# The first block's output projection with weights and operands split in high and low parts, in place of unsplit float32

## The chip, the cores and the metric

One core of a Trainium2 chip runs the whole program in one launch. The metric is the device time in microseconds; the kernel before has a median of 1708.94 us over 3 runs (1707.21 to 1710.25).

## The reference

A sequence of 256 tokens of width 1024, in float32, goes through two transformer-like blocks. The part that the change touches is the end of the first mixer of the first block:

```
y_a = gelu(z_gate) * rg_lru(xr, ...)                 # 256 x 1024, eight heads of 128
y_b = multi_scale_pool(z_pool, ...)                  # 256 x 512, four groups of 128
x = x + concatenate([y_a, y_b], axis=-1) @ w_out     # w_out is 1536 x 1024
```

Behind it come cross-attention (queries, scores, mix, output projection `wo0`), a gated feed-forward with a convolution, a conformer convolution block, a second cross-attention and feed-forward, and a second block with banded attention and a mixture of experts.

## The kernel before

All activations lie transposed: 128 channels on the partitions, 256 tokens along the free axis, so a tensor of width 1024 is eight chunks of 128x256. The weights come as one long stream of slabs, each 128x1024 float32 (512 KB), which SyncE loads into a ring of 12 places (`raw`). `S0` gives the first slab of each phase: `abin` (slab 0), `gk` (20), `v0` (32), `about` (40), `q0` (52), `wo0` (60). `about` is the output projection in question, with 12 slabs: the first four for the four pool groups, the other eight for the eight heads of the recurrence. A row slab holds 128 rows of the weight matrix; it gives eight products 128x128 by 128x256, one for each output chunk, which accumulate over the slabs of the phase in the eight half banks of `acc`.

**Two ways of multiplying.** For most phases ScalarE copies the raw slab to `wh` as float32r, the high part (line 699), and VectorE (line 1199) or GpSimd (line 1082) subtracts it from the raw slab to give `wl`, the low part: VectorE for slabs with an even split number, GpSimd for odd ones. The operand is in two parts in the same way (`yh` and `yl` for row slabs). TensorE then makes three float32r products for each float32 product, high by high, low by high and high by low (`tile3`, lines 1957 to 1959). `wh` and `wl` have four places (`SPLIT`), so a split waits until TensorE is done with the slab four back; splits are issued three slabs ahead (`AHEAD`). The phases `abin`, part of `gk`, `about` and `cw` are not split: `tile1` (line 1963) multiplies `raw` by the float32 operand, and the profile shows two records for each such product.

**The order around the change.** Every engine runs its own list in order, and they meet at counting semaphores. In the value phase `v0`, TensorE works on slabs 32 to 39. The first half (32 to 35) accumulates in banks `acc[2]` and `acc[3]`, which VectorE copies out in `v0_out(0)` (line 1370); the projection may not start before, as it uses the same banks:

```
            pe.wait_ge(S("v0_out"), TT)
            for n in range(12):
```

Meanwhile VectorE finishes the recurrence, one head after the other: a multiply (L1403), a scan (L1405) and a multiply with the gate (L1408), which leaves `y_a` of head n in `xr[:, n, :]` and raises `ya_ready`. `v0_out(0)` comes after head 4, `v0_out(1)` (line 1368) after head 7; in between stand the weight subtractions of slabs 36 and 38. `y_b` is in `z[:, 16 + g, :]` much earlier. In the projection TensorE waits for the raw slab and the operand alone; ScalarE, VectorE and GpSimd do little there except for the splits of slabs 52 to 54. When the last slab's chunks are done, VectorE adds them to the residual (`take_sums`, line 1253), ScalarE makes high parts `ah` of the next operand (L706), VectorE the low parts, and TensorE goes on with the first three query slabs (`lead`, lines 2042, 2043 and 2032). `row_slab`, the routine for split row slabs, runs already in `wo0` and later phases.

SyncE loads slab s into the place of slab s - 12: if that one is split, once its low part is made, otherwise once TensorE is done with it.

Of the kernel before, what the change touches and what calls it, by code (L numbers as in the profile page):

```python
# [31 lines left out]
F32 = mybir.dt.float32  # L32
# [206 lines left out]
def unsplit(s):  # L239

    if S0["gk"] <= s < S0["v0"]:
        return (s - S0["gk"]) % 3 == 0
    return s < S0["gk"] or S0["about"] <= s < S0["q0"] or S0["cw"] <= s < S0["cw"] + CW


def split_no(s):

    if s < S0["v0"]:
        return s - S0["gk"] - (s - S0["gk"] + 2) // 3
    if s < S0["about"]:  # L250
        return s - S0["gk"] - 4
    return s - S0["gk"] - 4 - 12 - (0 if s < S0["cw"] else CW)

# [62 lines left out]
def program(nc, stream, experts, cols_in, konst_in, masks_in, x_in, mem_in, router_in, out):  # L316
    ctx = ExitStack()
    with ctx:
# [366 lines left out]
        def _(act):  # L685
            A = Program(act, S("scalar_chain"))

            def split(s):
# [4 lines left out]
                if S0["v1"] <= s.base < S0["v1"] + SPLIT:  # L693
                    wait_slab(act, s + -(SPLIT + CW))
                elif S0["q0"] <= s.base < S0["q0"] + SPLIT:
                    wait_slab(act, s + -(SPLIT + 12))
                elif s.base >= S0["gk"] + SPLIT:
                    wait_slab(act, s + -SPLIT)
# [84 lines left out]
            for n in range(8):  # L783
                if n < 7:
                    split(At(S0["v0"] + n + 1 + AHEAD))
            for n in range(8):
                split(At(S0["about"] + n + AHEAD))
            act.dma_start(masks[:], masks_in).then_inc(S("masks_in"), 16)
# [285 lines left out]
        def _(pool):  # L1074
# [45 lines left out]
            splits(S0["gk"], 12)  # L1120
            splits(S0["v0"], 8)
            splits(S0["about"], 12)
# [68 lines left out]
        def _(dve):  # L1191
# [219 lines left out]
            v0_out(1)  # L1411
            splits(S0["about"], 11)
            take_sums("about")
# [539 lines left out]
        def _(pe):  # L1953
# [353 lines left out]
            for n in range(12):  # L2307
                s = At(S0["about"] + n)
                wait_raw(pe, s)
                if n < 4:  # L2310
                    wait_emptied(pe, USE0["gk"] + 5 * n + 2)
                else:
                    pe.wait_ge(S("ya_ready"), n - 3)
                for c in range(KC):
                    last = tile1(acc_of(c), s, c, z[:, 16 + n, :] if n < 4 else xr[:, n - 4, :],
                                 n == 0 and c % 2 == 0, n == 11, skip_group_check=True)
                    if n == 11 and c < KC - 1:
                        last.then_inc(acc_full, 1)
                last.then_inc(slab_done, 1)

# [505 lines left out]
```

## Time and profile before

| | us |
|---|---|
| median of 3 runs | 1708.94 |
| lowest, highest | 1707.21, 1710.25 |
| the profiled execution | 1709.44 |
| its span in the profile | 1707.6 |
| TensorE busy | 1635.0 (96%) |
| VectorE, ScalarE, GpSimd busy | 833.2, 603.8, 472.2 |
| unsplit matmuls of the projection (one piece of the chain) | 41.57 |

The span runs from the first to the last instruction that the profile shows. In the rows below PE is TensorE's matmuls, PEld its weight loads, DVE is VectorE, ACT ScalarE, POOL GpSimd, SP SyncE; L1963 is line 1963 of the kernel; `out<-in` names what is written and read; a time in brackets is how long the engine sat idle before the instruction, and what released it. Matmul records overlap, as they are pipelined, so the pace is the distance of two starts.

### The profile page before, as it was taken

What the parts mean: (1) busy time and instruction counts of PE and PEld (TensorE: products, weight loads), DVE (VectorE), ACT (ScalarE), POOL (GpSimd) and SP (SyncE); (2) the same over time, 40 slices, a digit from 0 to 9 for tenths busy, and PEclk for the clock granted to TensorE, in tenths of its full rate; (3) what the DMA queues carried; (4) which work ended last, traced back from release to release, by engine and by line L of the source; (5) the groups of instructions that cost most, each with busy time, mean ns of one, the idle gap of its engine ahead of it and who ended that gap; (6) DMA issues with size and microseconds to landing.
All of it is one profiled execution on the core that took longest, in us unless ns stands there. A gap on an engine that the chain in (4) does not pass through costs nothing.

```text
span 1707.6 us, 29356 instructions
## 1 busy us (share of the span) xinstructions
PE 1635.0 (96%) x11462; PEld 1294.7 (76%) x11462; DVE 833.2 (49%) x1397; ACT 603.8 (35%) x1019; POOL 472.2 (28%) x257
## 2 busy tenths in 40 slices
PE   7999999999999999999999999998799999999996
PEld 6898999999998799899999988887744443434332
DVE  2664457788873463888885436766501011010102
ACT  2371453443542444534444334655211111111101
POOL 1331424555543142355555342221200000000000
PEclk9999999999999999999999999999899999999998
DMA  7464634555568453455535664232979999999995
GB/s 290 149 222 154 212 109 149 185 172 184 185 177 247 165 182 118 138 180 181 177 127 161 228 190 136 98 104 102 370 297 421 421 421 422 422 421 422 421 422 212
DMA packets 85773, 401.06 MB, mean 235 GB/s; under 512 B 9520, under 2 KB 14000, under 8 KB 60848
## 3 DMA queue, kind: packets, MB, share of 16 engines
q1 hardware_dynamic: 84672, 395.81, 62.9%
q10 hardware_dynamic: 1008, 3.96, 0.6%
q8 instruction: 65, 1.06, 0.3%
q14 instruction: 28, 0.23, 0.0%
HBM read 394.02 MB, written 1.05 MB: 231 GB/s over the span
## 4 chain that ended last, share of the span: by engine, by line
PE 40%; issue 31%; DVE 23%; ACT 4%; POOL 1%; DVEq 1%; DMA 0%; ACTq 0%; SPq 0%; POOLq 0%
DVE wl L1199 5%; DVE cf L1517 5%; PE pw L1957 5%; PE pw L1959 5%; PE pw L1958 5%; PE pw L2270 4%; DVE hid L1533 3%; ACT wh L699 3%; DVE cf L1520 3%; PE acc L1963 2%; PE acc L1957 2%; PE acc L1959 2%; PE acc L1958 2%; PE acc L2129 2%; DVE gpad L1511 1%
## 5 line engine op out<-in xcount | busy, mean ns | idle before, releaser
L1082 POOL TENSOR_TENSOR wl<-raw,wh 128x1024 fp32r<-128x1024 f32 x157 | 388.3, 2474 | 579.9 <-ACT wh L699 576.2
L699 ACT ACTIVATE wh<-raw 128x1024 fp32r<-128x1024 f32 x314 | 325.0, 1051 | 245.3 <-PE pw L1959 108.5
L1957 PE MATMUL pw<-ah,wh 128*128 128x256 f32 x1272 | 364.4, 287 | 7.5 <-DVE gt L1690 4.0
L1958 PE MATMUL pw<-ah,wl 128*128 128x256 f32 x1272 | 359.8, 283 | 0.0
L1959 PE MATMUL pw<-al,wh 128*128 128x256 f32 x1272 | 359.7, 283 | 0.0
L1199 DVE TENSOR_TENSOR wl<-raw,wh 128x1024 fp32r<-128x1024 f32 x157 | 202.2, 1288 | 126.0 <-ACT wh L699 125.6
L1957 PEld LDWEIGHTS pw<-ah,wh 128*128 128x128 f32 x1272 | 243.6, 192 | 12.8 <-issue 10.5
L1958 PEld LDWEIGHTS pw<-ah,wl 128*128 128x128 f32 x1272 | 243.9, 192 | 0.1
L1959 PEld LDWEIGHTS pw<-al,wh 128*128 128x128 f32 x1272 | 243.8, 192 | 0.0
L1957 PE MATMUL acc<-yh,wh 128*128 128x256 f32 x672 | 194.8, 290 | 6.9 <-DVE yl L1729 2.8
L1958 PE MATMUL acc<-yh,wl 128*128 128x256 f32 x672 | 191.3, 285 | 0.0
L1959 PE MATMUL acc<-yl,wh 128*128 128x256 f32 x672 | 191.2, 285 | 0.0
L1093 POOL TENSOR_TENSOR small<-small 128x2 f32<-128x2 f32 x12 | 12.0, 1002 | 549.2 <-DVE small L1216 544.9
L1957 PEld LDWEIGHTS acc<-yh,wh 128*128 128x128 f32 x672 | 129.9, 193 | 10.0 <-issue 4.2
L1958 PEld LDWEIGHTS acc<-yh,wl 128*128 128x128 f32 x672 | 130.1, 194 | 0.1
L1959 PEld LDWEIGHTS acc<-yl,wh 128*128 128x128 f32 x672 | 130.0, 193 | 0.0
L1908 DVE COPY slot_gate<-pw 64x1 f32<-64x1 f32 x32 | 5.0, 156 | 245.7 <-ACT slots_to_tokens L1029 245.2
L2526 PE MATMUL pw<-raw,gathered 128*64 128x512 f32 x408 | 96.5, 601 | 3.5 <-DMA raw<-in_experts 2.0
L1517 DVE TENSOR_SCALAR cf<-gpad,cols 128x256 f32<-128x256 f32 x48 | 90.3, 1881 | 7.5 <-DVE gpad L1511 6.9
L2270 PE MATMUL pw<-x_gained,raw 128*128 128x256 f32 x320 | 74.4, 394 | 8.6 <-DMA raw<-in_stream 8.6
L852 ACT ACTIVATE cf<-cf 128x256 f32<-128x256 f32 x48 | 20.1, 418 | 164.5 <-DVE cf L1520 164.2
L1151 POOL TENSOR_TENSOR yl<-hid,yh 128x256 fp32r<-128x256 f32 x48 | 50.1, 1044 | 96.9 <-ACT yh L856 96.9
(315 smaller groups left out, 2601.8 us busy)
## 6 DMA issues: line engine op xcount, KB each, us to landing
raw<-in_stream SPq DMA_DIRECT2D x358, 512.0 KB, 3.3
raw<-in_experts SPq DMA_DIRECT2D x72, 1024.0 KB, 24.8
ring_w<-in_experts SPq DMA_DIRECT2D x47, 1024.0 KB, 26.7
ring_y<-in_experts SPq DMA_DIRECT2D x36, 1024.0 KB, 24.7
ring_m<-in_experts SPq DMA_DIRECT2D x24, 1024.0 KB, 24.8
ring_h<-in_experts SPq DMA_DIRECT2D x11, 1024.0 KB, 27.5
shifted<-hpad SPq DMA_DIRECT2D x16, 177.5 KB, 4.6
mem_t<-in_mem ACTq DMA_DIRECT2D x2, 1024.0 KB, 9.2
```

The lines of the kernel that those rows point to most:

```text
L699: A.done(act.activation(wh[:, s.base % SPLIT, :], raw[:, slot_of(s.base), :], ACT.Copy), w_hi)
L1082: G.done(pool.tensor_tensor(wl[:, s.base % SPLIT, :], raw[:, slot_of(s.base), :], wh[:, s.base % SPLIT, :].bitcast(F32), ALU.subtract), w_ ...
L1151: G.done(pool.tensor_tensor(yl[:, j % 4, :], hid[:, j % 2, :], yh[:, j % 4, :].bitcast(F32), ALU.subtract), S("ffn_hid_lo"))
L1199: V.done(dve.tensor_tensor(wl[:, s.base % SPLIT, :], raw[:, slot_of(s.base), :], wh[:, s.base % SPLIT, :].bitcast(F32), ALU.subtract), w_lo_v)
L1517: V.done(dve.tensor_scalar(cf[:, j % 2, :], gpad[:, j % 2, 2:T + 2], w, col(f"f_dw_b{l}", j, 4, i), ALU.mult, ALU.add))
L1520: V.done(dve.scalar_tensor_tensor(cf[:, j % 2, :], gpad[:, j % 2, 2 - k:T + 2 - k], w, cf[:, j % 2, :], ALU.mult, ALU.add), S("ffn_conv") ...
L1533: V.done(dve.tensor_tensor(hid[:, j % 2, :], cf[:, j % 2, :], uf[:, j % 2, :], ALU.mult), S("ffn_hidden"))
L1957: pe.matmul(dst, wh[:, s.base % SPLIT, w], hi, start=start, stop=False, **kw)
L1958: pe.matmul(dst, wl[:, s.base % SPLIT, w], hi, start=False, stop=False, **kw)
L1959: return pe.matmul(dst, wh[:, s.base % SPLIT, w], lo, start=False, stop=stop, **kw)
L2270: last = pe.matmul(pw[u % 4][:, 0:T], raw[:, slot_of(n), k * P:k * P + P], ax[:, k, :], start=(k == 0), stop=(k == KC - 1))
L2526: ins = pe.matmul(pw[bank + h][rows, :], stationary(e), expert_pair(s.base - S0["moe"])[:, e, 512 * h:512 * h + 512], start=first, stop=la ...
```

## The change

The twelve slabs of `about` are no longer exempt from splitting, and TensorE uses `row_slab` for them. ScalarE makes the high parts `yh` of the operands: of the four pool groups during the value phase, of the eight heads as they come, each followed by a weight split. GpSimd makes the low parts `yl` of the four pool groups, between its weight subtractions; VectorE makes those of the eight heads after `v0_out(1)`. The weight subtractions of slabs 40 to 51 go to VectorE (even) and GpSimd (odd), at the places where the lists call `split`: VectorE's of slab 40 stands before head 4, that of slab 42 before head 6. The load of the masks stays behind the same loop on ScalarE's queue, which has work in it now.

```diff
--- before.py
+++ after.py
@@ -240,16 +240,14 @@
 
     if S0["gk"] <= s < S0["v0"]:
         return (s - S0["gk"]) % 3 == 0
-    return s < S0["gk"] or S0["about"] <= s < S0["q0"] or S0["cw"] <= s < S0["cw"] + CW
+    return s < S0["gk"] or S0["cw"] <= s < S0["cw"] + CW
 
 
 def split_no(s):
 
     if s < S0["v0"]:
         return s - S0["gk"] - (s - S0["gk"] + 2) // 3
-    if s < S0["about"]:
-        return s - S0["gk"] - 4
-    return s - S0["gk"] - 4 - 12 - (0 if s < S0["cw"] else CW)
+    return s - S0["gk"] - 4 - (0 if s < S0["cw"] else CW)
 
 
 def ffn0(name):
@@ -692,8 +690,6 @@
                 wait_raw(act, s)
                 if S0["v1"] <= s.base < S0["v1"] + SPLIT:
                     wait_slab(act, s + -(SPLIT + CW))
-                elif S0["q0"] <= s.base < S0["q0"] + SPLIT:
-                    wait_slab(act, s + -(SPLIT + 12))
                 elif s.base >= S0["gk"] + SPLIT:
                     wait_slab(act, s + -SPLIT)
                 A.done(act.activation(wh[:, s.base % SPLIT, :], raw[:, slot_of(s.base), :], ACT.Copy), w_hi)
@@ -783,7 +779,12 @@
             for n in range(8):
                 if n < 7:
                     split(At(S0["v0"] + n + 1 + AHEAD))
+                if n < 4:
+                    wait_emptied(act, USE0["gk"] + 5 * n + 2)
+                    A.done(act.activation(yh[:, n, :], z[:, 16 + n, :], ACT.Copy), S("ab_hi"))
             for n in range(8):
+                act.wait_ge(S("ya_ready"), n + 1)
+                A.done(act.activation(yh[:, 4 + n, :], xr[:, n, :], ACT.Copy), S("ab_hi"))
                 split(At(S0["about"] + n + AHEAD))
             act.dma_start(masks[:], masks_in).then_inc(S("masks_in"), 16)
 
@@ -1118,7 +1119,12 @@
                     G.fence()
                     G.done(pool.tensor_tensor(z[:, 16 + g, :], src, z[:, 16 + g, :], ALU.subtract), S("pooled"))
             splits(S0["gk"], 12)
-            splits(S0["v0"], 8)
+            for n in range(8):
+                split(At(S0["v0"] + n + AHEAD))
+                if 1 <= n < 5:
+                    pool.wait_ge(S("ab_hi"), n)
+                    G.done(pool.tensor_tensor(yl[:, n - 1, :], z[:, 15 + n, :], yh[:, n - 1, :].bitcast(F32), ALU.subtract),
+                           S("ab_lo_pool"))
             splits(S0["about"], 12)
             for n in range(KC):
                 split(At(S0["q0"] + n + AHEAD))
@@ -1409,7 +1415,12 @@
                 if n == 4:
                     v0_out(0)
             v0_out(1)
-            splits(S0["about"], 11)
+            for n in range(11):
+                if n < 8:
+                    dve.wait_ge(S("ab_hi"), 5 + n)
+                    V.done(dve.tensor_tensor(yl[:, 4 + n, :], xr[:, n, :], yh[:, 4 + n, :].bitcast(F32), ALU.subtract),
+                           S("ab_lo_vector"))
+                split(At(S0["about"] + n + AHEAD))
             take_sums("about")
             split(At(S0["about"] + 11 + AHEAD))
 
@@ -2305,18 +2316,11 @@
                     value_slab(At(S0["v0"] + 4 * half + kk), kk, banks, mh, ml)
             pe.wait_ge(S("v0_out"), TT)
             for n in range(12):
-                s = At(S0["about"] + n)
-                wait_raw(pe, s)
                 if n < 4:
-                    wait_emptied(pe, USE0["gk"] + 5 * n + 2)
+                    pe.wait_ge(S("ab_lo_pool"), n + 1)
                 else:
-                    pe.wait_ge(S("ya_ready"), n - 3)
-                for c in range(KC):
-                    last = tile1(acc_of(c), s, c, z[:, 16 + n, :] if n < 4 else xr[:, n - 4, :],
-                                 n == 0 and c % 2 == 0, n == 11, skip_group_check=True)
-                    if n == 11 and c < KC - 1:
-                        last.then_inc(acc_full, 1)
-                last.then_inc(slab_done, 1)
+                    pe.wait_ge(S("ab_lo_vector"), n - 3)
+                row_slab(At(S0["about"] + n), n, n == 0, n == 11)
 
             def cross_layer(l):
                 lead(f"q{l}", f"xa{l}", f"q{l}")
```

## Rows read from the trace of the kernel before

**Rows 1.** The page, its first rows: span, busy time, share and instructions of TensorE.

```profile
span 1707.6 us, 29356 instructions
...
PE 1635.0 (96%) x11462; PEld 1294.7 (76%) x11462; DVE 833.2 (49%) x1397; ACT 603.8 (35%) x1019; POOL 472.2 (28%) x257
```

**Rows 2.** The chain that ended last, 100 to 200 us: start, duration, what.

```profile
142.19 41.57 PE acc L1963 x192
```

**Rows 3.** The waits, 120 to 190 us: who waited for whom, total, times, longest (us).

```profile
PEld acc L1963 <- DVE v_m L1370: 0.3, 1, 0.3
```

**Rows 4.** Timeline of TensorE, 131 to 257 us: start us, us, engine, line, op, out<-in, count.

```profile
131.15 0.39 PE L2091 MATMUL pw<-wh,mh 128*128 128x512 f32 x1
...
136.59 0.39 PE L2091 MATMUL pw<-wh,mh 128*128 128x512 f32 x1
...
142.05 14.08 PE L1963 MATMUL acc<-z,raw 128*128 128x256 f32 x64
...
183.41 0.47 PE L2042 MATMUL pw<-ah,wh 128*128 128x256 f32 x1
...
189.39 1.12 PE L2032 MATMUL pw<-al,wh 128*128 128x256 f32 x8
...
226.86 0.47 PE L1957 MATMUL acc<-yh,wh 128*128 128x256 f32 x1
...
250.08 0.28 PE L2042 MATMUL pw<-ah,wh 128*128 128x256 f32 x1
...
256.13 1.12 PE L2032 MATMUL pw<-al,wh 128*128 128x256 f32 x8
```

**Rows 5.** Timeline of VectorE, 122 to 142 us (same columns).

```profile
122.05 0.42 DVE L1334 COPY k_t<-pw 128x256 f32<-128x256 f32 x1
...
127.56 2.77 DVE L1405 TENSOR_TENSOR_SCAN z<-a_t,xr 128x256 f32<-128x256 f32 x1
...
131.35 0.69 DVE L1405 TENSOR_TENSOR_SCAN z<-a_t,xr 128x256 f32<-128x256 f32 x1
...
132.42 1.22 DVE L1199 TENSOR_TENSOR wl<-raw,wh 128x1024 fp32r<-128x1024 f32 x1
...
133.74 2.44 DVE L1403 TENSOR_TENSOR xr<-xr,z 128x256 f32<-128x256 f32 x1
...
139.19 0.43 DVE L1403 TENSOR_TENSOR xr<-xr,z 128x256 f32<-128x256 f32 x1
...
140.71 1.28 DVE L1370 COPY v_m<-acc 128x512 f32<-128x512 f32 x2
```

**Rows 6.** Timeline of GpSimd, 121 to 289 us (idle time and its releaser in brackets).

```profile
121.64 2.75 POOL L1082 TENSOR_TENSOR wl<-raw,wh 128x1024 fp32r<-128x1024 f32 x1 [2.92 <-ACT wh L699]
...
127.11 2.68 POOL L1082 TENSOR_TENSOR wl<-raw,wh 128x1024 fp32r<-128x1024 f32 x1 [2.72 <-ACT wh L699]
...
132.54 3.35 POOL L1082 TENSOR_TENSOR wl<-raw,wh 128x1024 fp32r<-128x1024 f32 x1 [2.76 <-ACT wh L699]
...
268.20 0.74 POOL L1151 TENSOR_TENSOR yl<-hid,yh 128x256 fp32r<-128x256 f32 x1 [3.39 <-ACT yh L856]
...
288.94 1.47 POOL L1151 TENSOR_TENSOR yl<-hid,yh 128x256 fp32r<-128x256 f32 x1 [2.98 <-ACT yh L856]
```

**Rows 7.** Timeline of ScalarE: a weight split, and an operand's high part.

```profile
125.97 1.06 ACT L699 ACTIVATE wh<-raw 128x1024 fp32r<-128x1024 f32 x1 [0.23 <-PE acc L2093]
...
267.70 0.42 ACT L856 ACTIVATE yh<-hid 128x256 fp32r<-128x256 f32 x1 [0.57 <-DVE hid L1533]
```

**Rows 8.** Timeline of TensorE: the first records after its two longest idle times.

```profile
8.59 5.71 PE L2270 MATMUL pw<-x_gained,raw 128*128 128x256 f32 x16 [8.59 <-DMA raw<-in_stream]
...
1230.15 0.63 PE L2502 MATMUL acc<-chosen,router_konst 128*128 128x32 f32 x2 [5.22 <-DVE chosen L1865]
```

**Rows 9.** Busy time of each engine by stretch, with TensorE's granted clock (PEclk), 1228 to 1230 us.

```profile
core 0: us, PE busy (x) PEld busy (x) DVE busy (x) ACT busy (x) POOL busy (x), PEclk, DMA share, GB/s
1228.00:1230.00 2.00, 0.00 (x0) 0.00 (x0) 1.97 (x15) 0.00 (x0) 0.00 (x0) 0.50 1.00 418
```

## The prediction

> **What bounds the kernel now.** The page comes first: TensorE is busy for 1635.0 of 1707.6 us [rows 1], so time is won or lost only where TensorE's own work or a gap in it changes. The chain that ended last, asked for the stretch of the output projection, gives one piece: 192 records of the unsplit matmul, 41.57 us without a break [rows 2]. A 128x256 float32 product leaves two records, so these are 12 slabs of 8 products, 0.433 us each. The waits name one stop at its door: TensorE waited 0.3 us for VectorE's copies out of the value sums [rows 3]. That small row matters most. The projection accumulates in the banks that these copies empty, and the copies stand in VectorE's queue behind five heads of the recurrence. VectorE had no slack there, and the change puts work in front of them.
>
> **TensorE's own work.** The row-slab routine already runs in the next projection: its eight slabs take 226.86 to 250.08 us. The first record is drawn out, so I go by records 0.12 us apart: 24 per slab, 2.88 us [rows 4]. Before, the run from 142.05 to 183.41 us [rows 4] gives 3.45 us a slab. Twelve slabs: 41.36 - 34.56 = 6.8 us gained, if everything arrives in time. A rule weighed against this: the Trainium skill (FP8 and Floating Point Precision, TensorE Precision Notes) says that true float32 takes 4 passes through the array. Counted as passes, three instead of four would give 31.0 us and a gain of 10.3, so the forecast below would be 3.5 us lower. The rows disagree: three split records cost 0.36 us against 0.433, a ratio of 0.83, and I keep the rows.
>
> **What is added to VectorE ahead of the value copies.** Calling the slabs of this projection 40 to 51 and the value slabs 32 to 39, VectorE now subtracts the low weights of slab 40 before head 4 (and those of 42 before head 6). One such subtraction is 1.22 us [rows 5], with its gap 1.3.
>
> **What GpSimd does to VectorE.** GpSimd gets four low parts of the pool operands and the low weights of slabs 41 and 43 in the same stretch. In the trace these operations and VectorE's operations with both inputs in SBUF exclude each other. The scan at 127.56 took 2.77 us and the multiply at 133.74 took 2.44, against 0.69 and 0.42 free, each ending 0.3 to 0.5 us after GpSimd's subtraction [rows 5, 6]. The reverse holds too: GpSimd's op at 132.54 took 3.35 us because VectorE's 132.42 was in flight. A copy out of PSUM at 122.05 ran in 0.42 us inside GpSimd's 121.64 to 124.39 and is not held. So a weight subtraction on GpSimd costs VectorE 2.0 us if it falls among the heads. An operand's low part is 0.74 us free and 1.47 when held [rows 6]; by the same reckoning (duration less 0.35) it costs VectorE 0.4.
> Do they fall there? ScalarE splits a slab 0.26 us after TensorE leaves the slab four back, for 1.06 us [rows 7]; value slabs last 2.72 us (131.15 to 142.05 for four [rows 4]). Slab 41 is ready for GpSimd at 136.59 + 0.26 + 1.06 = 137.9. Slab 43 waits for slab 39: with the small stop below, about 143.1 + 1.3 = 144.4. VectorE is then still in heads 2 to 4, so both hold it. The four operand parts come at 126 to 136 us, after ScalarE's 0.42 us copies [rows 7], and meet heads too.
> Sum: 1.3 + 2 x 2.0 + 4 x 0.4 = 6.9 us. Each of the ten or so handovers opens a few hundredths, and I take 7.2. The copies end at 140.71 + 1.28 + 7.2 = 149.2 instead of 142.0 [rows 5], and TensorE starts the projection 7.2 us late. The bounds: 1.3 if GpSimd's ops miss the heads or cost nothing, 9 if a third weight subtraction gets in.
>
> **A stop inside the value slabs.** The low weights of slab 38 began at 132.42. Three operand parts and the subtraction of slab 39 now come in ahead: 3 to 4 us later, done at 137.3 to 137.7, against 136.59, when TensorE wants them [rows 4]. That is 0.7 to 1.1 us, but it lies inside the 7.2, since TensorE then waits for the value copies anyway.
>
> **While the projection runs.** Per two slabs (5.76 us) GpSimd has 2.4 us, VectorE 1.22 + 2 x 0.42, together 4.5 when they exclude each other; ScalarE 2 x 1.48. Each fits. The first tight point is slab 44, whose operand VectorE makes only after heads 5 to 7 (3 x 1.7), slab 42 (1.3), the second pair of value copies (1.3), two operand parts (0.9), slab 44 itself (1.3) and one hold (2.0): 11.9 us after 149.2, so 161.1, where TensorE arrives at 149.25 + 4 x 2.88 = 160.8. A stop of 0 to 0.3 us, which the next term covers. The matmuls now wait for these low parts; nothing else on TensorE could run ahead of them.
>
> **The clock.** TensorE stands idle for some 6 us (143.1 to 149.2), longer than the 5.22 us before the router's counting [rows 8], where the granted clock stood at 0.50, the 1.2 GHz level, just before work resumed [rows 9]; and the first sixteen records of the kernel, after 8.59 us idle, took 5.71 us [rows 8], where 0.2165 us a record [rows 2] would give 3.46. That is 2.2 us lost there. I take 1.8, since fewer records of the shorter kind come first; the bounds are 0 and 3.5 (the full idle here is shorter, but nothing says how fast the clock returns).
>
> **The far end.** The three lead slabs of the queries, fed by the sums through VectorE and ScalarE, took 183.41 to 189.39 after the unsplit slab, and 250.08 to 256.13 after a split one [rows 4]: 0.07 us more. The four-back waits of ScalarE for slabs 51 to 54 end 1.3 us into the last slab, just ahead of the first sum. SP's loads of slabs 52 to 63 now follow the split of the slab in their slot, at about 145 for the first, where slab 40's end (145.5) released it; no later, and the splits of 52 come 30 us after. ScalarE's load of the masks slips from 131 to past 170 us; they are used only by the second block's attention. ScalarE was idle there, and its 12 splits and 12 copies (12 x 1.48 us) fit.
>
> **Sum.** 7.2 - 6.8 + 0.07 + 1.8 = +2.3 us. The profiled execution took 1709.44 us; it becomes 1711.7. That run lies 0.5 above the median of 1708.94, so I forecast 1711.2 for the median. Nothing behind absorbs a shift: TensorE goes straight on.
>
> **Rivals.** A measurement here can tell about 0.2%, 3.4 us.
> - *The forecast*: late value copies eat the gain. 1711.2, its own range 1709.5 to 1713. Chance 0.45, of which 0.08 lies past 1712.4.
> - *The clock does not fall, or only one of the two weight subtractions holds VectorE*: 2 us less each, 1707.5 to 1709.5. For it: both prices come from other places of the kernel. Against it: the two idles of rows 8 both left a mark. 0.20, within 0.2%.
> - *Slower, through the clock*: after the idle, TensorE stays at the lower level for 3.5 us more than it would, and slabs 44 to 46 come late too because GpSimd holds VectorE again. It decides once more than 2.8 us are lost to clock and stops together: 7.2 - 6.8 + 0.07 + 3.5 + 1 = +5, 1713.9. For it: at 1228 to 1230 the clock had already fallen with the idle [rows 9]. The Trainium skill (TensorE: Matmul & The Clock Gate, Part 1) calls the throttled state the default that activity releases, which agrees with that row. 0.25.
> - *Faster*: GpSimd's operations slip past the heads (they meet the copies, which are not held), the value copies end 1.3 us late, and the gain of 6.8 stands: 1.3 - 6.8 + 0.1 = -5.4, 1703.5. Against it: three of three weight subtractions on GpSimd in rows 6 met a VectorE op. 0.10.
> That the split matmuls would not run as such is excluded: the routine is the one of rows 4.
>
> **Numbers.** Faster 0.10; slower 0.25 + 0.08 = 0.33; the same 0.57. The range 1706.8 to 1714.8 takes in the second case and most of the third, and leaves out the fourth and a tail above.
>
> **What would show it.** Right: TensorE's wait for the value copies (before: 0.3 us) is 5 to 7 us, the copies end near 149 us, VectorE's ops among the heads show 2 us and more four times instead of twice, twelve slabs at 2.88 us after the first, a granted clock of 0.5 somewhere in 147 to 153. Wrong: a projection that starts before 145 us (then the kernel is faster), waits for low weights beyond slab 44 of more than a microsecond in sum (then slower), or a slab spacing other than 2.88.

## The result and the profile after

The changed kernel takes 1712.30 us in the median of 15 runs (1710.62 to 1713.55), beside 1709.21 for 15 runs of the kernel before (1707.21 to 1711.46). The ratio is 1.0016 [1.0009, 1.0023], or +3.1 us, slower by a little less than the 0.2% named in the prediction. The forecast was +2.3 us. A second comparison later gave 1.0010 [1.0001, 1.0019], or +1.7 us. The profiled execution took 1711.19 us, 1.8 us more than the profiled one before.

The page of the changed kernel answers to [rows 1]:

```profile
span 1709.4 us, 29608 instructions
PE 1630.8 (95%) x11558; PEld 1295.8 (76%) x11558; DVE 854.6 (50%) x1411; ACT 620.1 (36%) x1043; POOL 491.2 (29%) x267
```

TensorE is busy for 4.2 us less and the span is 1.8 us longer, so about 6 us of new idle time must lie somewhere. The waits of TensorE between 120 and 195 us (in total, times, longest, in us) name it:

```profile
PE acc L1968 <- DVE v_m L1376: 5.8, 1, 5.8
PE pw L2102 <- DVE wl L1205: 0.6, 1, 0.6
```

In place of the 0.3 us of [rows 3] TensorE waits 5.8 us for the value copies, and 0.6 us for the low weights of slab 38. No other wait of this stretch ended on low parts. TensorE's timeline shows both, and what follows (start, duration, line, operation, and in brackets the idle time and its releaser):

```profile
136.18 0.50 PE L2102 MATMUL pw<-wh,mh 128*128 128x512 f32 x1 [0.56 <-DVE wl L1205]
...
141.53 0.39 PE L2104 MATMUL pw<-wh,ml 128*128 128x512 f32 x1
147.75 0.58 PE L1968 MATMUL acc<-yh,wh 128*128 128x256 f32 x1 [5.83 <-DVE v_m L1376]
148.13 0.41 PE L1969 MATMUL acc<-yh,wl 128*128 128x256 f32 x1
...
150.48 0.38 PE L1968 MATMUL acc<-yh,wh 128*128 128x256 f32 x1
150.69 0.28 PE L1969 MATMUL acc<-yh,wl 128*128 128x256 f32 x1
150.81 0.28 PE L1970 MATMUL acc<-yl,wh 128*128 128x256 f32 x1
...
183.69 0.28 PE L2053 MATMUL pw<-ah,wh 128*128 128x256 f32 x1
```

This execution reached the stretch early: the low weights of slab 36 are made at 124.64, against 125.77 us before. So 1.13 us has to be added to its times to compare them. The head start arose ahead of anything that the change touches: the execution before shows a granted clock of 0.50 from 36.6 to 40.0 us, where that of the changed kernel shows 1.00.

```profile
36.60:40.00 3.40, 3.40 (x10) 2.64 (x9) 0.98 (x4) 0.60 (x1) 1.54 (x3) 0.50 0.39 133
```

The line gives the window, its length, the busy times of PE, PEld, DVE, ACT and POOL with their instructions, the granted clock, the busy share of the DMA engines and GB/s.

The projection starts at 147.75 + 1.13 = 148.88, against 142.05 before [rows 4], 6.8 us late. Its first twelve records are 0.21 to 0.38 us apart (2.73 us in all), the rest 0.12. It lasts 183.69 - 147.75 = 35.94 us, against 41.36 [rows 4]: 5.4 less. The stage as a whole is thus 6.8 - 5.4 = 1.4 us longer.

VectorE's timeline answers to [rows 5] and GpSimd's to [rows 6]. The first is VectorE's:

```profile
125.98 0.78 DVE L1409 TENSOR_TENSOR xr<-xr,z 128x256 f32<-128x256 f32 x1
126.79 2.77 DVE L1411 TENSOR_TENSOR_SCAN z<-a_t,xr 128x256 f32<-128x256 f32 x1
129.59 0.78 DVE L1414 TENSOR_TENSOR xr<-z 128x256 f32<-128x256 f32 x1
130.48 0.78 DVE L1409 TENSOR_TENSOR xr<-xr,z 128x256 f32<-128x256 f32 x1
...
132.01 2.44 DVE L1414 TENSOR_TENSOR xr<-z 128x256 f32<-128x256 f32 x1
134.38 1.75 DVE L1205 TENSOR_TENSOR wl<-raw,wh 128x1024 fp32r<-128x1024 f32 x1
...
137.42 2.44 DVE L1414 TENSOR_TENSOR xr<-z 128x256 f32<-128x256 f32 x1
...
141.50 1.22 DVE L1205 TENSOR_TENSOR wl<-raw,wh 128x1024 fp32r<-128x1024 f32 x1
142.82 0.43 DVE L1409 TENSOR_TENSOR xr<-xr,z 128x256 f32<-128x256 f32 x1
143.28 2.76 DVE L1411 TENSOR_TENSOR_SCAN z<-a_t,xr 128x256 f32<-128x256 f32 x1
146.07 0.42 DVE L1414 TENSOR_TENSOR xr<-z 128x256 f32<-128x256 f32 x1
146.42 1.28 DVE L1376 COPY v_m<-acc 128x512 f32<-128x512 f32 x2
```

And GpSimd's, with the low parts of the operands (L1126) among the weights (L1083):

```profile
126.44 2.58 POOL L1083 TENSOR_TENSOR wl<-raw,wh 128x1024 fp32r<-128x1024 f32 x1
128.96 2.00 POOL L1126 TENSOR_TENSOR yl<-z,yh 128x256 fp32r<-128x256 f32 x2
131.42 2.75 POOL L1083 TENSOR_TENSOR wl<-raw,wh 128x1024 fp32r<-128x1024 f32 x1 [0.46 <-ACT wh L695]
134.13 0.92 POOL L1126 TENSOR_TENSOR yl<-z,yh 128x256 fp32r<-128x256 f32 x1
136.86 2.72 POOL L1083 TENSOR_TENSOR wl<-raw,wh 128x1024 fp32r<-128x1024 f32 x1 [1.82 <-ACT wh L695]
143.15 2.34 POOL L1083 TENSOR_TENSOR wl<-raw,wh 128x1024 fp32r<-128x1024 f32 x1 [3.57 <-ACT wh L695]
```

Each of these weight subtractions on GpSimd has a stretched operation of VectorE beside it. Those of slabs 41 (136.86) and 43 (143.15) are new, and hold a multiply for 2.44 - 0.42 = 2.02 us and a scan for 2.76 - 0.69 = 2.07. The low parts of operands hold it for less: the multiplies at 125.98, 129.59 and 130.48 take 0.78 each where their like takes 0.42, and the subtraction at 134.38 takes 1.75 where others take 1.22.

The windows of the changed kernel show the granted clock behind the five busy times: 0.50, the 1.2 GHz level, while the projection starts, and 1.00, the 2.4 GHz level, for the rest of it.

```profile
147.26:150.68 3.42, 2.93 (x13) 2.93 (x14) 3.14 (x6) 0.00 (x0) 0.00 (x0) 0.50 0.02 5
150.70:183.60 32.90, 32.90 (x276) 32.90 (x276) 21.12 (x27) 14.92 (x21) 12.55 (x5) 1.00 0.61 207
```

### The profile page after: what moved, and what is told of

It reads as the page before. It is cut to its first block, busy times and chain, and to the rows that moved or that the text cites. A ratio compares the mean times of both kernels' runs of the same rounds, so it can differ in the third digit from the quotient of the medians.

```text
span 1709.4 us, 29608 instructions
## 1 busy us (share of the span) xinstructions
PE 1630.8 (95%) x11558; PEld 1295.8 (76%) x11558; DVE 854.6 (50%) x1411; ACT 620.1 (36%) x1043; POOL 491.2 (29%) x267
## 4 chain that ended last, share of the span: by engine, by line
PE 39%; issue 31%; DVE 24%; ACT 4%; POOL 1%; DVEq 1%; DMA 0%; ACTq 0%; SPq 0%; POOLq 0%
DVE wl L1205 6%; DVE cf L1528 5%; PE pw L1968 5%; PE pw L1969 5%; PE pw L1970 5%; PE pw L2281 4%; DVE hid L1544 3%; ACT wh L695 3%; PE acc L1968 3%; DVE cf L1531 3%; PE acc L1970 3%; PE acc L1969 3%; PE acc L2140 2%; DVE gpad L1522 1%; PE pw L2053 1%
## 5 line engine op out<-in xcount | busy, mean ns | idle before, releaser
L1083 POOL TENSOR_TENSOR wl<-raw,wh 128x1024 fp32r<-128x1024 f32 x163 | 402.9, 2472 | 561.8 <-ACT wh L695 558.1
L695 ACT ACTIVATE wh<-raw 128x1024 fp32r<-128x1024 f32 x326 | 337.8, 1051 | 256.5 <-PE pw L1970 108.7
L1205 DVE TENSOR_TENSOR wl<-raw,wh 128x1024 fp32r<-128x1024 f32 x163 | 210.1, 1290 | 130.1 <-ACT wh L695 129.4
L1968 PE MATMUL acc<-yh,wh 128*128 128x256 f32 x768 | 222.9, 290 | 12.8 <-DVE v_m L1376 5.8
L1969 PE MATMUL acc<-yh,wl 128*128 128x256 f32 x768 | 219.2, 285 | 0.0
L1970 PE MATMUL acc<-yl,wh 128*128 128x256 f32 x768 | 219.1, 285 | 0.0
L1968 PEld LDWEIGHTS acc<-yh,wh 128*128 128x128 f32 x768 | 148.7, 194 | 16.2 <-DVE v_m L1376 6.3
L1969 PEld LDWEIGHTS acc<-yh,wl 128*128 128x128 f32 x768 | 149.0, 194 | 0.1
L1970 PEld LDWEIGHTS acc<-yl,wh 128*128 128x128 f32 x768 | 148.9, 194 | 0.0
```

Source lines behind the costliest of these rows:

```text
L695: A.done(act.activation(wh[:, s.base % SPLIT, :], raw[:, slot_of(s.base), :], ACT.Copy), w_hi)
L1083: G.done(pool.tensor_tensor(wl[:, s.base % SPLIT, :], raw[:, slot_of(s.base), :], wh[:, s.base % SPLIT, :].bitcast(F32), ALU.subtract), w_ ...
L1205: V.done(dve.tensor_tensor(wl[:, s.base % SPLIT, :], raw[:, slot_of(s.base), :], wh[:, s.base % SPLIT, :].bitcast(F32), ALU.subtract), w_lo_v)
L1968: pe.matmul(dst, wh[:, s.base % SPLIT, w], hi, start=start, stop=False, **kw)
L1969: pe.matmul(dst, wl[:, s.base % SPLIT, w], hi, start=False, stop=False, **kw)
L1970: return pe.matmul(dst, wh[:, s.base % SPLIT, w], lo, start=False, stop=stop, **kw)
```

## The experiments

The change was taken apart in three ways: the pace of the matmuls alone, the side work alone, and the side work of one engine at a time. Then came versions that repair the order, and last a question that the first runs had raised, about the time behind the stage. For every kernel the profile gives the **stage**, from the first matmul of the value slabs (120.2 us before) to the first query matmul (183.4), and the **rest**, from there to the end of the span. Stage and rest come from one profiled execution of each kernel, and the median from several executions, beside that of the kernel before, measured along with it; so a median is compared with the one in its brackets and not with another row's.

| kernel | stage, us | rest, us | median (before's beside it) | ratio |
|---|---|---|---|---|
| before | 63.2 | 1524.2 | | |
| changed | 64.6 | 1525.7 | 1712.30 (1709.21) | 1.0016 [1.0009, 1.0023] |
| pace_only | 56.4 | 1524.6 | 1704.24 (1709.65) | 0.9968 [0.9957, 0.9979] |
| side_only | 71.8 | 1523.9 | 1720.48 (1709.65) | 1.0060 [1.0046, 1.0074] |
| copies_early | 64.5 | 1524.9 | 1709.94 (1709.65) | 1.0001 [0.9992, 1.0010] |
| reordered | 58.5 | 1525.3 | 1706.33 (1709.65) | 0.9979 [0.9969, 0.9988] |
| kept_busy | 63.4 | 1527.0 | 1712.74 (1709.40) | 1.0019 [1.0010, 1.0028] |
| gpsimd_short | 57.6 | 1524.5 | 1705.08 (1709.40) | 0.9974 [0.9963, 0.9985] |
| heads_only | 60.8 | 1527.3 | 1711.65 (1709.40) | 1.0013 [1.0004, 1.0022] |
| after_again | 64.6 | 1526.0 | 1711.35 (1709.62) | 1.0010 [1.0001, 1.0019] |
| before_pad12 | 64.8 | 1531.9 | 1714.41 (1709.62) | 1.0027 [1.0018, 1.0036] |
| before_pad24 | 66.2 | 1526.6 | 1714.04 (1709.62) | 1.0035 [1.0021, 1.0049] |
| reordered_2 | 57.4 | 1526.1 | 1704.94 (1709.62) | 0.9975 [0.9966, 0.9984] |

### The matmuls' pace alone: pace_only

The kernel before, with three products on parts that lie ready, and no side work for them:

```diff
                 elif S0["q0"] <= s.base < S0["q0"] + SPLIT:
-                    wait_slab(act, s + -(SPLIT + 12))
+                    wait_slab(act, s + -SPLIT)
...
-                    last = tile1(acc_of(c), s, c, z[:, 16 + n, :] if n < 4 else xr[:, n - 4, :],
+                    last = tile3(acc_of(c), s, c, mh[:, n % 8, :], ml[:, n % 8, :],
```

> The kernel before, with split matmuls in the projection but none of the new side work: TensorE multiplies what lies in the weight halves from earlier slabs and the memory operand's parts, so the projection's values are not computed. Theory (the matmuls gain 6.8 us, the side work ahead of the value copies loses it): twelve slabs at 2.88 us from 142 us without a stop, 6.8 us less than before, 1702.4 us. Rival (the split matmuls are no faster in this place): within 1 us of before, 1709.

The first query matmuls come at 176.2 us. One row of their line (count, shortest, median and longest duration in ns, first and last start):

```profile
L2042 PE MATMUL pw<-ah,wh x24: 278/283/387, 176.2 to 182.0; 128*128 128x256 f32 x24
```

The projection starts at 141.55 without a wait and lasts 34.65 us, and the stage is 63.2 - 56.4 = 6.8 us shorter, what the distance of the records gave. The median shows 5.4 us of it (1709.65 - 1704.24), and the interval, -7.3 to -3.6 us, takes in the whole. By the ratio of the two durations, 34.65 to 41.36 or 0.84, three split products are dearer than three quarters of an unsplit one. The Trainium skill (FP8 and Floating Point Precision, TensorE Precision Notes) counts true float32 as four passes. By its count the estimate would be 31.0 us, and no run shows that.

### The side work alone: side_only

The changed kernel, with all its splits and waits, but with the unsplit matmuls:

```diff
...
-                row_slab(At(S0["about"] + n), n, n == 0, n == 11)
+                s = At(S0["about"] + n)
+                wait_split(pe, s)
+                for c in range(KC):
+                    last = tile1(acc_of(c), s, c, z[:, 16 + n, :] if n < 4 else xr[:, n - 4, :],
...
```

> The changed kernel with all its splits and operand parts, but TensorE multiplies unsplit as before. Theory: the start of the projection is as late as in the changed kernel (6.8 us) and the clock falls in the wait (1.4 us): 8.2 us more than before, 1717.4 us, and 5 us more than the changed kernel. Rival (the side work is hidden and it is the split matmuls that wait): within 1 us of before.

TensorE's timeline at the start of the projection:

```profile
149.17 9.00 PE L1976 MATMUL acc<-z,raw 128*128 128x256 f32 x32 [5.83 <-DVE v_m L1378]
```

The wait is 5.83 us, as in the changed kernel, though the matmuls are the old ones. So the lateness comes from the side work and not from the split matmuls. The start is 28.6 us after the first value matmul (149.17 - 120.53), where before it was 21.8 (142.05 - 120.24): 6.8 us late. The stage grows by 8.6 us (8.2 had been expected) and the median by 10.8, more than the 8.2 expected of it. The other 1.8 us of the stage is what the projection takes longer than 41.36, and the clock accounts for it. The granted clock is 0.50 for the first 3.73 us of the projection, and 1.00 behind:

```profile
149.17:152.90 3.73, 3.73 (x9) 3.01 (x10) 3.48 (x6) 0.00 (x0) 0.00 (x0) 0.50 0.02 4
```

Half of 3.73 is 1.87. In the changed kernel the clock was back 2.9 us after the start (147.75 to 150.68), and cost 1.3 to 1.4. So the same idle of 5.83 us had two prices.

### GpSimd's part: gpsimd_short

GpSimd's new subtractions keep their places and waits, but work on four columns:

```diff
-                G.done(pool.tensor_tensor(wl[:, s.base % SPLIT, :], raw[:, slot_of(s.base), :],
-                                          wh[:, s.base % SPLIT, :].bitcast(F32), ALU.subtract), w_lo_p)
+                e = 4 if s.base in (41, 43) else SLAB
+                G.done(pool.tensor_tensor(wl[:, s.base % SPLIT, 0:e], raw[:, slot_of(s.base), 0:e],
+                                          wh[:, s.base % SPLIT, 0:e].bitcast(F32), ALU.subtract), w_lo_p)
...
-                    G.done(pool.tensor_tensor(yl[:, n - 1, :], z[:, 15 + n, :], yh[:, n - 1, :].bitcast(F32), ALU.subtract),
+                    G.done(pool.tensor_tensor(yl[:, n - 1, 0:4], z[:, 15 + n, 0:4], yh[:, n - 1, 0:4].bitcast(F32), ALU.subtract),
...
```

> The changed kernel in which GpSimd subtracts only 4 columns where it made the four pool operands' low parts and the low weights of slabs 41 and 43; TensorE multiplies with stale low weights there and with the high part in place of the operand's low part, so part of the low products is wrong. Theory (GpSimd's operations hold VectorE's, 2.0 and 0.4 us each): the value copies end 5.6 us earlier, TensorE's wait for them falls from 5.8 to 1.5 to 2 us, the clock does not fall, and the time is 6 to 7 us less than that of the changed kernel, 1705.5 to 1706.5 us. Rival (VectorE is late by its own work alone): less than 1.5 us less, 1711 us.

VectorE's timeline of this kernel, where slab 41's and slab 43's subtractions had held it:

```profile
138.35 1.22 DVE L1206 TENSOR_TENSOR wl<-raw,wh 128x1024 fp32r<-128x1024 f32 x1
139.67 0.43 DVE L1410 TENSOR_TENSOR xr<-xr,z 128x256 f32<-128x256 f32 x1
140.13 0.69 DVE L1412 TENSOR_TENSOR_SCAN z<-a_t,xr 128x256 f32<-128x256 f32 x1
140.86 0.43 DVE L1415 TENSOR_TENSOR xr<-z 128x256 f32<-128x256 f32 x1
141.20 1.28 DVE L1377 COPY v_m<-acc 128x512 f32<-128x512 f32 x2
```

No operation of VectorE between the last weight subtraction ahead of the copies and the copies is held. They end at 142.48 us, which is 22.9 us after the first value matmul (119.6). In the changed kernel it is 147.70 - 119.1 = 28.6, and before it was 141.99 - 120.2 = 21.8. The 5.7 us between the first two are GpSimd's whole share, and equal the sum of the stretched rows: 2.02 + 2.07 for the weights and 3 x 0.36 + 0.53 = 1.6 for the operands. TensorE's wait falls to 1.0 us (1.5 to 2 had been expected) and the stage to 57.6; the median, 1705.08, lies 0.4 us below the expected range. This settles the cause: of the 6.8 us, 5.7 are VectorE standing still for GpSimd, and the other 1.1 its own subtraction of slab 40.

The Trainium skill (SBUF — State Buffer, Who interferes with whom) says that a VectorE operation with both inputs in SBUF and a GpSimd operation that reads SBUF share an interface, and that whichever comes first keeps the other out altogether. The rows agree, with 2.02 to 2.07 us for a subtraction over 128x1024. That copies out of PSUM are not held is seen where they run inside a subtraction of GpSimd's, as in reordered_2 below: they take their 1.28 us there too.

### The clock: kept_busy

TensorE runs 44 products of no use into a free bank while it would wait for the copies:

```diff
+            wait_emptied(pe, USE0["v0"] - 2)
+            for n in range(44):
+                pe.matmul(pw[(USE0["v0"] + 2) % 4][:, 0:T], mh[:, n % 8, 0:P], mh[:, n % 8, :], start=True, stop=True)
             pe.wait_ge(S("v0_out"), TT)
```

> The changed kernel with 44 further products (of parts that lie there anyway, into an idle bank, 5.3 us in all) on TensorE between the value slabs and its wait for the value copies. Theory: 1.4 us of the loss are the clock, which falls in the idle: the granted clock stays at 1.00 and the time is 1.4 us less than that of the changed kernel, 1710.9 us. Rival (the clock costs nothing, the pace after the wait has another reason): no difference, 1712.3, and slow first slabs as before.

The timeline of TensorE, and below it the window in which the changed kernel had stood at 0.50:

```profile
142.49 5.43 PE L2319 MATMUL pw<-mh 128*128 128x256 f32 x44
148.54 0.38 PE L1968 MATMUL acc<-yh,wh 128*128 128x256 f32 x1 [0.62 <-DVE v_m L1376]
148.77 0.28 PE L1969 MATMUL acc<-yh,wl 128*128 128x256 f32 x1
148.88 0.28 PE L1970 MATMUL acc<-yl,wh 128*128 128x256 f32 x1
```

```profile
147.00:151.00 4.00, 3.38 (x28) 3.18 (x27) 3.83 (x7) 0.00 (x0) 0.00 (x0) 1.00 0.09 37
```

The clock stays at 1.00, the records are 0.12 us apart from the second on, and the stage is 1.2 us shorter than the changed kernel's: the projection takes 34.65 us, as in pace_only, against 35.94. The price of the idle in the stage is therefore 1.2 to 1.4 us. But nothing of it is seen in the total: 1712.74, ratio 1.0019, with a rest of 1527.0 us. As an expectation of the total this one missed.

### The copies earlier: copies_early

`v0_out(0)` comes two heads earlier; the low weights that had stood before head 4 now stand before head 3:

```diff
-                if n < 7:
+                if n < 7 and n != 4:
                     split(At(S0["v0"] + n + 1 + AHEAD))
+                if n == 3:
+                    split(At(S0["v0"] + 4 + 1 + AHEAD))
...
-                if n == 4:
+                if n == 2:
                     v0_out(0)
```

> The changed kernel with the first pair of value copies after head 2 in place of head 4, and the low weights of slab 40 ahead of head 3 in place of head 4. Theory (VectorE's whole queue is late, the copies are only where it shows first): TensorE starts the projection 5 to 6 us earlier but then waits about 5 us for the low weights of slab 42, which stand behind heads 3 to 5, and 1 us at slab 44; the end of the projection moves by less than 1.5 us, and the time is 1710.5 to 1712.5. Rival (the copies are the one bottleneck): the whole 7 us come back, 1704 to 1705 us.

The waits of TensorE in the stage:

```profile
PE acc L1970 <- DVE wl L1205: 5.2, 3, 2.4
PE pw L2104 <- DVE wl L1205: 0.6, 1, 0.6
```

The projection starts 23.2 us after the first value matmul, 5.4 earlier than in the changed kernel. The wait for the copies is gone, and three waits for low weights, 5.2 us together, have taken its place: 0.4 us at slab 40, 2.3 at slab 42 and 2.5 at slab 44, where about 5 at slab 42 and 1 at slab 44 had been expected. The stage is 64.5 us against 64.6. So moving the copies alone brings nothing to the stage: the heads that no longer stand ahead of the copies now stand ahead of low weights that TensorE needs as soon. The median, 1709.94, lies 0.6 us below the expected range. It is 0.3 us above that of the kernel before beside it, where the changed kernel's was 3.1 and 1.7 above; with the stages equal, the stage does not explain the difference.

### Half of the slabs: heads_only

The four pool slabs stay unsplit, the eight head slabs are split:

```diff
-    return s < S0["gk"] or S0["cw"] <= s < S0["cw"] + CW
+    return s < S0["gk"] or S0["about"] <= s < S0["about"] + 4 or S0["cw"] <= s < S0["cw"] + CW
...
```

> Only the eight slabs of the heads are split; the four of the pool groups stay unsplit float32. No low weights of 40 to 43 and no pool operand parts in front of the heads, but GpSimd's low weights of slab 45 (and perhaps 47) still fall among them. Theory: 8 x 0.57 = 4.5 us gained by TensorE, 2 us lost at the value copies per weight subtraction of GpSimd that meets the heads: 1706.5 to 1707.5 us. Rival (GpSimd costs VectorE nothing): 1704.7 us.

With four slabs more before the first low part is needed, TensorE waits 1.9 us for the copies, and the stage is 60.8 us, 2.4 us shorter than before. What the expectation says of the stage holds (4.5 gained, 2 lost); that for the total missed widely: 1711.65, ratio 1.0013. The rest is 1527.3 us, 3.1 more than before.

### Another order: reordered and reordered_2

VectorE's and ScalarE's lists for this stretch were written out anew, by when TensorE needs each result. Heads 3 to 7 move behind the copies, and the weights stand where their deadlines are:

```diff
+VECTOR_ORDER = [("weights", 36), ("head", 0), ("weights", 38), ("head", 1), ("head", 2), ("copies", 0),
+                ("weights", 40), ("weights", 42), ("head", 3), ("low", 0), ("low", 1), ("weights", 44),
+                ("head", 4), ("head", 5), ("low", 2), ("low", 3), ("head", 6), ("weights", 46), ("head", 7),
+                ("low", 4), ("low", 5), ("weights", 48), ("copies", 1), ("low", 6), ("low", 7),
+                ("weights", 50), ("weights", 52)]
...
+            for kind, n in VECTOR_ORDER:
+                if kind == "weights":
+                    split(At(n))
+                elif kind == "head":
+                    head(n)
...
```

> The changed kernel with VectorE's list put in the order in which TensorE needs its results (low weights of 38 ahead of head 1, value copies after head 2, low weights of 40 and 42 next, each head's low part soon after it, the second value copies late) and ScalarE's list to match. Theory: VectorE's work is only badly ordered, not too much: no stop above 1 us, no idle for the clock to fall in, 6 to 7 us less than before, 1702 to 1703.5 us. Rival (VectorE and GpSimd together have too much work in this stretch whatever the order): stops move behind slab 42, 1707 us or more.

It is faster than both kernels, by 3.3 us against the one before, but it missed the 1702 to 1703.5 expected. One wait of 1.4 us was left, for the low weights of slab 40, which stood behind head 2 and the copies. The second version swaps them:

```diff
-VECTOR_ORDER = [("weights", 36), ("head", 0), ("weights", 38), ("head", 1), ("head", 2), ("copies", 0),
-                ("weights", 40), ("weights", 42), ("head", 3), ("low", 0), ("low", 1), ("weights", 44),
+VECTOR_ORDER = [("weights", 36), ("head", 0), ("weights", 38), ("head", 1), ("weights", 40), ("copies", 0),
+                ("head", 2), ("weights", 42), ("head", 3), ("low", 0), ("low", 1), ("weights", 44),
```

> The reordered kernel with the low weights of slab 40 and the value copies ahead of head 2, and those of slab 42 behind it. Theory: the stop of 1.4 us at slab 40 goes, the stage is 1 to 1.4 us shorter than in the reordered kernel, and the time 1705 to 1705.5 us. Rival (the stop moves to slab 42 or 46): no difference, 1706.3 us.

The waits of TensorE, and VectorE's timeline around the copies:

```profile
PE acc L1984 <- DVE wl L1216: 0.6, 2, 0.3
```

```profile
137.23 1.22 DVE L1216 TENSOR_TENSOR wl<-raw,wh 128x1024 fp32r<-128x1024 f32 x1
138.37 1.28 DVE L1387 COPY v_m<-acc 128x512 f32<-128x512 f32 x2
139.75 1.25 DVE L1418 TENSOR_TENSOR xr<-xr,z 128x256 f32<-128x256 f32 x1
```

GpSimd's subtraction of slab 41 runs beside them:

```profile
137.99 2.74 POOL L1094 TENSOR_TENSOR wl<-raw,wh 128x1024 fp32r<-128x1024 f32 x1 [1.68 <-ACT wh L706]
```

The low weights of slab 40 and the copies both come before TensorE asks; the stage is 57.4 us, 5.8 below before and 1.0 above what pace_only shows as the floor, and 1.1 below reordered, as expected. The median is 1704.94, ratio 0.9975 [0.9966, 0.9984]: 4.7 us below the kernel before, with the whole split projection in it. It is the fastest by its stage of the kernels that compute all of it; the totals of the two orders are not apart, as their intervals overlap. GpSimd still holds VectorE. But the copies run inside its subtraction of slab 41 unheld, so that subtraction holds the multiply behind them for 0.8 us (1.25 against 0.42) and not for 2.0, and behind the later holds TensorE waits 0.3 us at most.

### The time behind the stage: after_again, before_pad12, before_pad24

Some totals had not followed the stage. Is a microsecond lost in the stage a microsecond in the total? The changed kernel was run again, and the kernel before with 12 and with 24 products of no use behind the projection (0.12 us each, 1.4 and 2.9 us):

```diff
+            wait_emptied(pe, USE0["v0"] - 2)
+            for n in range(12):
+                pe.matmul(pw[(USE0["v0"] + 2) % 4][:, 0:T], mh[:, n % 8, 0:P], mh[:, n % 8, :], start=True, stop=True)
+
             def cross_layer(l):
```

> The changed kernel unchanged, once more. In its profile the stage from the value slabs to the queries was 1.4 us longer than before, while its median was 3.1 us higher. Theory A (the rest is a fixed property of the program, such as where its phases fall): again 3 us, 1712 us. Theory B (the rest is chance of the runs): 1 to 2 us, 1710 to 1711 us.

> The kernel before with 12 further products (1.44 us) on TensorE between the projection and the queries: the stage gets as much longer as in the changed kernel, with nothing else changed. Theory A (the time behind the stage depends on when it is reached, through the granted clock in the router's stage and at the tail): the total moves by clearly more or less than 1.4 us. Theory B: by 1.4 us, 1710.9 us.

> The same with 24 products (2.88 us). Theory A: again not in proportion. Theory B: 2.9 us more than before, 1712.3 us.

The changed kernel comes out at 1711.35, +1.7 us, between the two theories. With the pads the stage grows by 1.6 and 3.0 us, as it should. The medians grow by 4.8 and 4.4 us; by the intervals of the ratios it is 3.1 to 6.2 us for 12 products and 3.6 to 8.4 for 24. So 12 products cost about twice their length or more, and the runs do not say which of the two pads costs more. The same comparison, interval against stage, gives a surplus clear of the noise for kept_busy (1.7 to 4.8 us, stage +0.2) and heads_only (0.7 to 3.8, stage -2.4); for pace_only, side_only, copies_early, gpsimd_short, reordered and after_again the stage lies inside the interval, and for the first comparison of the changed kernel (1.5 to 3.9, stage +1.4) and reordered_2 (-5.8 to -2.7, stage -5.8) at its edge. The table follows five points of the profiled executions through the program, in us against the kernel before, whose own times stand in the first line:

| kernel | query lead | lead at 902 | router | first streamed expert product | last expert product | end |
|---|---|---|---|---|---|---|
| before | 183.4 | 901.8 | 1217.3 | 1244.6 | 1691.0 | 1707.6 |
| changed | +0.3 | +0.4 | +2.6 | +4.2 | +1.8 | +1.8 |
| after_again | +0.2 | +0.2 | +2.3 | +3.9 | +2.0 | +2.0 |
| before_pad12 | -0.4 | -0.8 | +3.6 | +5.1 | +4.2 | +7.3 |
| before_pad24 | +2.2 | +1.9 | +1.8 | +1.8 | +1.8 | +4.6 |
| kept_busy | -0.2 | -0.1 | +0.8 | +2.4 | +0.8 | +2.6 |
| pace_only | -7.2 | -7.2 | -6.5 | -4.8 | -6.8 | -6.8 |
| heads_only | -2.9 | -2.3 | -2.0 | -0.4 | -2.6 | +0.2 |
| reordered_2 | -5.8 | -5.7 | -3.7 | -2.1 | -3.9 | -3.9 |

(The profiled executions come to the stage at 118.2 to 120.5 us, so part of the first column is from ahead of it. And each row is one execution: that of before_pad12 was the slowest of its 11, 2.2 us above their median, and that of heads_only 1.8 us below its median.) Up to 902 us a shift is passed on to within 0.6 us. Between there and the first expert product every kernel here but before_pad24 loses 1.9 to 5.9 us against the one before. The expert stream gives those 0.9 to 2.4 of it back; in the kernel before the granted clock is 0.50 in it from 1681.8 to 1685.2 us, and 1.00 there in the changed one. The last stretch differs again: from the last expert product to the end it is 16.6 us in the kernel before and in the changed one, and 1.8 to 3.1 us more in both padded kernels, in kept_busy and in heads_only. That is where the profiled execution of kept_busy gave away more than the 1.2 us won in the stage. The windows over the first and the last of these stretches, of the kernel before:

```profile
902.00:1245.00 343.00, 317.17 (x2464) 288.26 (x2464) 192.78 (x439) 154.78 (x296) 101.58 (x44) 0.97 0.49 172
1691.00:1707.60 16.60, 6.71 (x44) 3.98 (x40) 8.78 (x23) 3.82 (x10) 0.69 (x1) 0.84 0.18 64
```

of the changed kernel:

```profile
902.00:1249.00 347.00, 320.78 (x2468) 291.94 (x2468) 193.34 (x440) 155.23 (x297) 102.01 (x44) 0.96 0.49 171
1693.00:1709.40 16.40, 6.44 (x42) 3.98 (x40) 8.78 (x23) 3.82 (x10) 0.69 (x1) 0.83 0.18 65
```

and of before_pad12:

```profile
901.00:1250.00 349.00, 323.28 (x2466) 293.74 (x2466) 193.08 (x439) 154.97 (x296) 101.69 (x44) 0.95 0.47 170
1695.00:1714.90 19.90, 7.83 (x44) 4.70 (x40) 8.77 (x23) 3.81 (x10) 0.69 (x1) 0.68 0.15 54
```

The work is the same to a few records (x2464 to x2468), but the busy time of TensorE is 3.6 and 6.1 us longer, and the mean granted clock is lower, 0.96 and 0.95 in place of 0.97. In before_pad24, which loses nothing there, the clock is 0.97 and TensorE busy for 317.27 us, as before. In the tail of before_pad12 the clock is 0.68 in place of 0.84, and the tail takes 3.1 us more; in before_pad24, kept_busy and heads_only it is 0.70, 0.76 and 0.67. (Lengths of stretches are those of the table; the windows begin and end near whole microseconds.) So in these profiles the surplus goes with time at the lower clock, and the pads show that such a surplus can come without any of the changed kernel's side work.

Whether the places of the low clock belong to the program or to the single execution is not shown. The two profiles of the changed kernel agree to 0.4 us at every point of the table. But before, before_pad12 and before_pad24 run the same instructions up to 183 us, and the clock is 0.50 from 36.6 to 40.0 in the first, 1.00 there and around it in the second, and 0.50 from 35.1 to 38.5 in the third; they come to the stage at 120.2, 118.2 and 119.4 us. Several profiles of one kernel would tell, and were not taken.

## Why the prediction was right

The forecast was the first case, late value copies that eat the gain, +2.3 us. Measured were +3.1 and +1.7 in the medians, and +1.8 in the profiled execution. Point by point, for the stage:

- **The gain of 6.8.** Shown by pace_only (41.36 - 34.65 = 6.7). The rule of four passes, weighed and set aside, would have put the forecast 3.5 us too low.
- **The copies 7.2 late.** Measured 6.8. The subtraction of slab 40 was taken at 1.3 and was worth 1.1. The two weight subtractions on GpSimd were taken at 4.0 and were 4.1. The four operand parts were taken at 1.6 and were 1.6. The 0.3 for the handovers was not needed. That the holds are the cause was argued from the rows, and gpsimd_short shows it.
- **The stop at slab 38**, 0.7 to 1.1: the slab starts at 136.18 + 1.13 = 137.31 against 136.59, 0.7 late, of which the profile shows 0.6 as idle. It lay inside the late start, as the step had it.
- **Slab 44 and behind**: no stop at all (0 to 0.3 had been allowed).
- **The clock 1.8**: the first twelve records took 2.73 us in place of 1.44, and all twelve slabs 35.94 in place of 34.56, so 1.4. The term was 0.4 too large for this run. That is not the length of the idle: side_only, with the same 5.83 us, lost 1.8. kept_busy shows in the stage that it is the clock.
- **The far end 0.07**: the three lead slabs take 6.04 us here, against 5.98.
- **"Nothing behind absorbs a shift: TensorE goes straight on."** This is the step that failed. The stage is 1.4 us longer, by 0.9 less than forecast, and the total by 1.7 to 3.1. Behind 902 us the execution first lost 3.8 us against the kernel before and then got 2.4 back. That the total came out near the forecast is partly luck: in the profiled execution -1.1 us from ahead of the stage, +1.4 in it and +1.5 behind it make the +1.8, and the prediction had +2.3 in the stage and nothing elsewhere.

Of the rivals, *the clock does not fall, or only one holds* is excluded by the 0.50 of its window and by the two holds of 2.02 and 2.07. *Slower through the clock* had 1713.9 on more than 2.8 us lost to clock and stops; 1.4 was lost. *Faster* is what gpsimd_short makes true: with the holds away the stage is 5.6 us shorter than before (5.4 in its sum), and 1705.08 is measured, 4.3 us below the kernel before beside it. It was priced well in the stage and did not happen. Against it the prediction counted three weight subtractions that met a VectorE operation; the rows show two that held one, as the first, at 121.64, had a copy out of PSUM beside it that ran in its 0.42 us.

## What to carry to other kernels

A faster matmul form brings only what the engines that feed it can deliver by its deadlines, so place each feeding operation in its queue by when TensorE needs its result: here that turned a stage 1.4 us longer than before into one 5.8 us shorter, and +3.1 or +1.7 us in the total into -4.7, with the same instructions. Price a GpSimd operation not only on its own queue but as a hold on whatever VectorE runs with two SBUF inputs beside it. And when a change is worth 1 to 3 us of 1700, read it from the stage that it touches, since the total can move by as much behind it.

## What was not expected of the hardware

That a small shift is not passed on one to one. Twelve products, 1.4 us, put in at 183 us, lengthened the kernel before by 4.8 us (1.0027 [1.0018, 1.0036]), and 24 did so by 4.4 (1.0035 [1.0021, 1.0049]). Between 902 us and the first expert product the same work took 343 to 349 us, at a granted clock of 0.97 to 0.95; the last stretch took 16.6 to 19.6 us, at 0.84 to 0.68. And that the same idle had two prices: after 5.83 us of it the clock stood at 0.50 for 2.9 us of the changed kernel's projection and for 3.7 us of side_only's. Keeping TensorE busy through the idle kept the clock at 1.00 there and shortened the stage by 1.2 us, and the total by nothing that shows.
